# A two-layer trunk on one core: the input projection's first four output tiles accumulated side by side, k outermost

## The reference

```python
def conv_pool_mixer(xn, w_in, ...):                  # layer 0
    proj = xn @ w_in                                 # 512 x 1024 by 1024 x 2048
    h, gate_b, gate_c, pin = jnp.split(proj, 4, axis=-1)
    ya = gate_b * causal_dwconv3(gate_c * h, conv_w)
    pooled = windowed means of pin (2, 4, 8, 16), less pin
    yb = pooled @ pool_w, per group of 128 channels, scaled
    return concatenate([ya, yb]) @ w_out

for layer in (0, 1):
    x = x + mixer(rmsnorm(x, g))                     # layer 1: dilated attention
    x = x + conv_glu_ffn(rmsnorm(x, g2))             # 1024 -> 5632 -> 2816 -> 1024
```

## Time and profile before

| | us |
|---|---|
| median of 3 runs | 1137.81 |
| lowest, highest | 1137.66, 1139.56 |
| the profiled execution: its time | 1137.77 |
| the profiled execution: its span | 1136.0 |

### The profile page before, as it was taken

One profiled execution on the slowest core, in us unless ns is written; L12 is line 12 of the kernel. 1 busy time (PEld: TensorE's weight loads), 2 busy tenths in 40 slices (PEclk: granted clock), 3 DMA queues, 4 the chain that ended last, 5 costly groups with the idle time before them and its releaser, 6 DMA issues.

```text
span 1136.0 us, 16020 instructions
## 1 busy us (share of the span) xinstructions
PE 1126.4 (99%) x5222; PEld 935.3 (82%) x5222; DVE 586.1 (52%) x1046; ACT 488.4 (43%) x750; POOL 460.8 (41%) x220
## 2 busy tenths in 40 slices
PE   8999999999999999999999999999999999999998
PEld 5788888888888888888888888878888888888887
DVE  6885755454454512215777777777844545450000
ACT  5323444444443432224666666544544444441220
POOL 3543534544435355542222233134544454435442
PEclk9999999999999999999999999999999999999999
DMA  7232323223222233332322223222332222323332
GB/s 247 78 125 77 111 74 112 92 92 111 84 101 84 63 112 93 99 113 65 91 83 78 74 74 99 77 74 77 127 106 81 108 92 92 95 63 102 102 98 77
DMA packets 35901, 108.11 MB, mean 95 GB/s; under 512 B 4192, under 2 KB 4192, under 8 KB 35872
## 3 DMA queue, kind: packets, MB, share of 16 engines
q1 hardware_dynamic: 33536, 103.49, 27.8%
q10 hardware_dynamic: 2336, 4.24, 1.3%
HBM read 105.57 MB, written 2.15 MB: 95 GB/s over the span
## 4 chain that ended last, share of the span: by engine, by line
issue 45%; PE 33%; POOL 20%; DMA 1%; POOLq 0%; ACT 0%; SPq 0%; DVE 0%; DVEq 0%
POOL wl L412 20%; PE bank L1040 7%; PE bank L1039 7%; PE bank L1038 7%; PE spt L1038 4%; PE spt L1039 4%; PE spt L1040 4%; DMA x<-xt 1%; POOLq L411 0%; POOLq L417 0%; ACT xh L452 0%; PE obank L1040 0%; PE obank L1039 0%; PE obank L1038 0%; ACT wh L442 0%
## 5 line engine op out<-in xcount | busy, mean ns | idle before, releaser
L412 POOL TENSOR_TENSOR wl<-raw,wh 128x1024 fp32r<-128x1024 f32 (+2 forms) x214 | 457.3, 2143 | 649.8 <-ACT wh L442 649.8
L1038 PE MATMUL bank<-xh,wh 128*128 128x512 f32 x1024 | 404.0, 395 | 1.9 <-DVE wl L749 1.9
L1040 PE MATMUL bank<-xh,wl 128*128 128x512 f32 x1024 | 399.8, 390 | 0.0
L1039 PE MATMUL bank<-xl,wh 128*128 128x512 f32 x1024 | 399.3, 390 | 0.0
L442 ACT ACTIVATE wh<-raw 128x1024 fp32r<-128x1024 f32 (+1 forms) x215 | 202.3, 946 | 144.1 <-PE spt L1040 139.5
L1038 PEld LDWEIGHTS bank<-xh,wh 128*128 128x128 f32 x1024 | 192.7, 188 | 42.4 <-DVE wl L749 2.8
L1040 PEld LDWEIGHTS bank<-xh,wl 128*128 128x128 f32 x1024 | 192.5, 188 | 40.2
L1039 PEld LDWEIGHTS bank<-xl,wh 128*128 128x128 f32 x1024 | 192.8, 188 | 38.6
L861 DVE TENSOR_TENSOR work<-bank,rstd 128x512 f32<-128x512 f32 x88 | 60.5, 691 | 225.7 <-PE bank L1040 223.8
L1038 PE MATMUL spt<-bh,wh 128*128 128x512 f32 x440 | 171.5, 390 | 0.4 <-POOL wl L412 0.3
L1039 PE MATMUL spt<-bl,wh 128*128 128x512 f32 x440 | 171.2, 389 | 0.0
(11 more groups left out here) (139 smaller groups left out, 887.0 us busy)
## 6 DMA issues: line engine op xcount, KB each, us to landing
raw<-w_up SPq DMA_DIRECT2D x88, 512.0 KB, 3.2
raw<-w_down SPq DMA_DIRECT2D x32, 384.0 KB, 3.1
raw<-w_down SPq DMA_DIRECT2D x32, 320.0 KB, 2.8
raw<-w_qkv SPq DMA_DIRECT2D x16, 512.0 KB, 3.4
raw<-w_in SPq DMA_DIRECT2D x15, 512.0 KB, 3.3
raw<-w_out SPq DMA_DIRECT2D x8, 512.0 KB, 3.2
raw<-w_qkv SPq DMA_DIRECT2D x16, 256.0 KB, 2.7
work<-bias_rows ACTq DMA_DIRECT2D x16, 256.0 KB, 3.1
```

The costliest lines, as they stand in the source:

```text
L412: nc.gpsimd.tensor_tensor(wl[s][:, 0:n], raw[s][:, 0:n], plain(wh[s][:, 0:n]), ALU.subtract).then_inc(s_lo, 1)
L1038: mm(dst, wh[s][:, w], hi, start=first, stop=False)
L1039: mm(dst, wh[s][:, w], lo, start=False, stop=False)
L1040: return mm(dst, wl[s][:, w], hi, start=False, stop=last)
```

## The change

**Loads.** x comes tile by tile (8 transfers of 256 KB). The first four units come k-wise: slot 0 holds k = 0 and 1 of tiles 0 to 3, slot 1 k = 2 and 3, and so on. The first four chunks (one k, four tiles, 256 KB) are single transfers whose rows are 512 B; slots 2 and 3 are loaded as pairs (512 KB, rows of 1 KB). x tiles and chunks alternate. The semaphores for halves become one per slot.

**TensorE.** Six warm-up matmuls of 256 columns instead of three of 512. For k = 0 to 5: four matmuls wh by xh into banks 0 to 3, four wh by xl, four wl by xh, each four with its own wait. Then, tile by tile, k = 6 and 7 (`first_end`). `norm_stats` stands after tile 0's end, `norm_spread` after tile 2's, the two bias products after tile 3's.

**The other engines.** VectorE rounds the very first chunk (`tensor_copy`) and forms its rest; ScalarE rounds the other chunks, GpSimd forms the other rests. ScalarE squares x tiles between its roundings; VectorE adds them between the rests of x, with the running sum in a PSUM bank (`first_acc`), and the last add goes to `acc`. ScalarE rounds unit 4 before the pooling weights and the norm's copy instead of after them. On VectorE the bias vectors and the pooling weights' rest move behind group 0; some memsets move to the start. The DMA of the bias rows on ScalarE's queue moves from group 0 to group 1. Some work buffers change places.

```diff
-WARM = 3
+WARM = 6
...
+        def chunk(buf, kk):
+            return buf[:].rearrange("p (j k n) -> p j k n", j=4, k=2)[:, :, kk, :]
...
+            def first_rows(k0, k1):
+                return w_in[0:4, :, k0 * P:k1 * P].rearrange("j p n -> p j n")
...
-            x_load(0)
-            sp.dma_start(raw[0][:, 0:SLOT // 2], w_in[0, :, 0:SLOT // 2]).then_inc(s_raw_a, 16)
-            load(0, 0, raw[0][:, SLOT // 2:], w_in[0, :, SLOT // 2:], True)
-            x_load(1)
-            load(1, 1, raw[1][:], w_in[1], True)
-            x_load(2)
-            x_load(3)
-            load(2, 2, raw[2][:], w_in[2], True)
+            for u in range(2):
+                x_load(2 * u)
+                half_load(u, 0, s_raw_a[u])
+                x_load(2 * u + 1)
+                half_load(u, 1, s_raw[u])
+            x_load(4)
+            pair_load(2)
+            x_load(5)
+            x_load(6)
+            pair_load(3)
+            x_load(7)
             sp.dma_start(par[:, C_FFN:], params[:, C_FFN:]).then_inc(s_par_b, 16)
-            load(3, 3, raw[3][:], w_in[3], True)
...
+            pool.wait_ge(s_hi, 1)
+            rest_first(0, 1).then_inc(s_lo, 1)
+            pool.wait_ge(s_hi_a[1], 1)
+            rest_first(1, 0).then_inc(s_lo_a[1], 1)
+            pool.wait_ge(s_hi, 2)
+            rest_first(1, 1).then_inc(s_lo, 1)
...
             round_first(0)
             round_first(1)
             act.wait_ge(s_raw[0], 16)
+            round_chunk(0, 1).then_inc(s_hi, 1)
+            square_first(0)
             round_first(2)
+            act.wait_ge(s_raw_a[1], 16)
+            round_chunk(1, 0).then_inc(s_hi_a[1], 1)
+            square_first(1)
             round_first(3)
+            act.wait_ge(s_raw[1], 16)
+            round_chunk(1, 1).then_inc(s_hi, 1)
+            square_first(2)
+            round_first(4)
             round_unit(0, 2, True)
+            square_first(3)
+            round_first(5)
+            square_first(4)
+            round_first(6)
+            round_unit(0, 3, True)
+            round_first(7)
+            for k in range(5, KT):
                 square_first(k)
+            ahead(U_IN, 0, 1)
...
+            dve.wait_ge(s_raw_a[0], 16)
+            nc.vector.tensor_copy(chunk(wh[0], 0), chunk(raw[0], 0)).then_inc(s_hi_a[0], 1)
             rest_x(0, 0)
+            dve.wait_ge(s_hi_a[0], 1)
+            nc.vector.tensor_tensor(chunk(wl[0], 0), chunk(raw[0], 0), plain(chunk(wh[0], 0)),
+                                    ALU.subtract).then_inc(s_lo_a[0], 1)
+            rest_x(0, 1)
+            for k in range(2, KT):
                 rest_x(0, k)
+                add_first(k - 2, first_acc)
+            add_first(KT - 2, first_acc)
             dve.wait_ge(s_warm, 1)
+            add_first(KT - 1, acc[:])
             norm_rsqrt(0)
...
-                last = mm(obank[:], acc[:, 0:P], acc[:], start=True, stop=True)
+                last = mm(obank[:, 0:SEQ // 2], acc[:, 0:P], acc[:, 0:SEQ // 2], start=True, stop=True)
...
+            for k in range(KT - 2):
+                early = k < 4 and k % 2 == 0
+                pe.wait_ge(s_xh, k + 1)
+                if early:
+                    pe.wait_ge(s_hi_a[k // 2], 1)
+                else:
+                    pe.wait_ge(s_hi, k // 2 + 1)
+                for j in range(4):
+                    mm(bank[j][:], first_weight(wh, j, k), xh[:, k, :], start=k == 0, stop=False)
+                pe.wait_ge(s_xl, k + 1)
+                for j in range(4):
+                    mm(bank[j][:], first_weight(wh, j, k), xl[:, k, :], start=False, stop=False)
+                if early:
+                    pe.wait_ge(s_lo_a[k // 2], 1)
+                else:
+                    unit_ready(U_IN + k // 2)
+                for j in range(4):
+                    last = mm(bank[j][:], first_weight(wl, j, k), xh[:, k, :], start=False, stop=False)
+                if k % 2:
                     last.then_inc(s_unit, 1)
...
+            pe.wait_ge(s_xl, KT)
+            unit_ready(U_IN + 3)
+            first_end(0)
             pe.wait_ge(s_par_b, 16)
             norm_stats(0)
+            first_end(1)
+            first_end(2)
+            norm_spread(0)
+            first_end(3)
             pe.wait_ge(s_setup, 48)
```

More of the change, by code:

```diff
@@ L221, in trunk @@
         s_warm = sem("s_warm")
-        s_xin = [sem(f"s_xin{n}") for n in range(4)]
+        s_xin = [sem(f"s_xin{n}") for n in range(KT)]
         s_pool = sem("s_pool")
@@ L372, in _ @@
             sp.dma_start(poolraw, poolw).then_inc(s_pool, 16)
-            sp.wait_ge(s_lo_a, 2)
+            for u in range(2):
+                sp.wait_ge(s_lo_a[u], 1)
             with sp.Fori(1, GROUPS) as i:
@@ L419, in rests, with rest_first @@
                         rest(i * RING + (first + s), s, sizes[s])
[L421 to L425, removed]
+            def rest_first(u, kk):
+                return nc.gpsimd.tensor_tensor(chunk(wl[u], kk), chunk(raw[u], kk), plain(chunk(wh[u], kk)),
+                                               ALU.subtract)
+            pool.wait_ge(s_hi, 1)
[4 more added lines that the diff above has]
+            rest_first(1, 1).then_inc(s_lo, 1)
             for s in range(2, RING):
@@ L499, in _ @@
                     ahead(U_IN, g, 0)
-                ahead(U_IN, g, 1)
+                    ahead(U_IN, g, 1)
                 act.wait_ge(s_zc, g + 1)
@@ L776, in _, with bias_vectors @@
[L776 to L784, removed]
-                                    ALU.subtract).then_inc(s_pwl, 1)
+            def bias_vectors():
+                dve.wait_ge(s_setup, 48)
+                dve.wait_ge(s_bvmm, 2)
+                heads = 2 * PAIRS
+                link(nc.vector.tensor_tensor(bv_sb[0:heads, 0:SEQ], obank[0:heads, :],
+                                             cnt_sb[0:heads, 0:SEQ], ALU.add))
+                nc.vector.tensor_tensor(bv_sb[0:heads, SEQ:NVEC], rbank[0][0:heads, 0:NVEC - SEQ],
+                                        cnt_sb[0:heads, SEQ:NVEC], ALU.add).then_inc(s_bv, 1)
+                dve.wait_ge(s_bv, 1)
+                link(nc.vector.memset(pb[:, 0:PAD], 0.0))
@@ L1083, in _ @@
             for n in range(WARM):
-                last = mm(obank[:], acc[:, 0:P], acc[:], start=True, stop=True)
+                last = mm(obank[:, 0:SEQ // 2], acc[:, 0:P], acc[:, 0:SEQ // 2], start=True, stop=True)
             last.then_inc(s_warm, 1)
-            def in_part(j, k0, k1):
-                for k in range(k0, k1):
-                    last = product(bank[j][:], j, k, xh[:, k, :], xl[:, k, :], k == 0, k == KT - 1)
-                if k1 == KT:
-                    last.then_inc(s_unit, 1)
@@ new lines, in first_end @@
+            def first_end(j):
+                for k in range(KT - 2, KT):
+                    mm(bank[j][:], first_weight(wh, j, k), xh[:, k, :], start=False, stop=False)
+                    mm(bank[j][:], first_weight(wh, j, k), xl[:, k, :], start=False, stop=False)
+                    last = mm(bank[j][:], first_weight(wl, j, k), xh[:, k, :], start=False, stop=k == KT - 1)
+                last.then_inc(s_first if j < 3 else s_unit, 1)
+            pe.wait_ge(s_xl, KT)
+            unit_ready(U_IN + 3)
```

100 lines of the change are left out of this document (42 added, 58 removed).

## The result

| | before | after |
|---|---|---|
| median, us | 1139.56 (7 runs) | 1132.62 (7 runs) |
| lowest to highest | 1137.66 to 1142.45 | 1132.41 to 1132.86 |
| the profiled execution, time and span | 1137.77, 1136.0 | 1132.44, 1130.6 |
| T1, first matmul of tile 4 | 36.96 | 31.61 |

The changed kernel takes 0.9942 of the time, 95% interval 0.9928 to 0.9955. Of the profiled executions it is 5.33 us shorter, and T1 is 5.35 us earlier: all of it is won in the opening and kept. By medians it is 6.9 us, since the kernel before scatters by 5 us and the changed one by half a microsecond.

The account below looks back on a forecast made before the run. TensorE's passage through the first four output tiles sets the time. T1 = 6.8 + 21.8 + 0.98 + 2.3 + 0.35 = 32.3, 4.66 us earlier (start 1.4, clock 1.8, waiting 1.8, less 0.35): 1133.1 us, range 1132.1 to 1136.0.

Parts of the forecast that it names:

- the fixed rest: Behind the statistics up to T1: two bias products, spread of the norm, longer steps; 2.3 us, expected to stay.
- The start: First projection matmul at 6.8 us instead of 8.23, set by first chunk landing at 6.2; 1.4 us gained.
- The 2 us allowed for uncovered weight loads: Warm-up: uncovered weight loads in the extra matmuls could add under 2 us to its expected end at 6.28.
- The packets: Opening loads: estimated 29 ns per 512 B packet and 47 ns per 1 KB, against 20 and 40.
- Rival (d): Opening loads: small k-wise packets become the bound, from 86 ns each T1 is past 36.96; 1141.1 us, chance 0.06.
- the kept clock: First ten projection matmuls: a shorter standstill ahead keeps TensorE's clock full; 1.8 us gained.
- the waiting that goes: TensorE at the sum of squares: its wait for VectorE's last add disappears; 1.8 us gained.
- rival (a): Opening: the clock still falls after a late first chunk, so 1.8 us are lost; 1134.9 us, chance 0.12.
- The sum of squares: VectorE's last add, helped by its PSUM operand, ends near 24.3, 0.2 us ahead of TensorE's statistics at 24.5.
- Rival (b): Late opening: GpSimd's unit 4 rest delays VectorE's xl by 1 us, last add by 0.7; 1134.8 us, chance 0.20.
- Cost nothing, under that cover: Bias vectors and pooling weights' rest behind group 0 on VectorE: no cost, 16.2 us against TensorE's 21.8 per group.
- Rival (c): Group 1: unit 5's rest, hanging on VectorE's group 0 work, takes up the gain; 1137.8 us, chance 0.07.

Follow-up runs that it names:

- The kernel with the clock kept: The kernel before with four warm-up matmuls of 512 columns instead of three, nothing else; median 1139.23 us, ratio 0.9999 to the kernel before.

## Why the prediction was right, and where a step of it was not

**T1 and the sum.** Predicted 32.3 for T1 and 1133.1 us; measured 31.61 and 1132.62 (1132.44 in the profiled execution). That the gain in the opening is kept whole was right: 5.35 us at T1, 5.33 us in the time. The sum of TensorE's own work held: 6.51 + 21.8 (96 steps) + 0.4 (the first matmul's step, 0.63 us instead of 0.23, the clock being still at half) + 0.8 (statistics) + 2.1 (the fixed rest, 25.45 to 31.61 less 18 steps) = 31.6. The statistics were given 0.98 and the fixed rest 2.3. The allowance of 0.35 for small waits was not needed.

**The start.** Predicted 6.8, measured 6.51, by another bound. The chunk was in by 5.28, not 6.2: from 2.2 to 4.0 us the queue moved 225 GB/s instead of the 193 of the earlier trace rows, which accounts for a part of it; the rest is not explained. The warm-up's end set the start. Its last pass began at 6.44 where that of the kernel before began at 5.68, since the clock rose only at 6.9 and not at 5.3. This moment changes from execution to execution: in two of the variants above with the same warm-up (the sum in SBUF, the bias vectors first) the clock rose at 4.6 and at 6.2, and the first matmul stood at 6.00 and at 6.36. That 6.51 lies so near to 6.8 is partly luck. The 2 us allowed for uncovered weight loads did not come: at half clock a pass of 256 columns takes 0.427 us and one of 512 columns 0.853. The packets came close to the estimate. The DMA view of the changed kernel from 5 to 9 us:

```profile
DMA packets 1463, 1.14 MB, mean 285 GB/s; under 512 B 69, under 2 KB 1185, under 8 KB 1463
...
q1 hardware_dynamic: 1463, 1.14, 97.5%
```

These are 1116 packets of 512 B, 278 of 2 KB and 69 small ones in 62 us of engine time (97.5% of 16 x 4). The times of the single packets in the trace are 27 ns for 512 B (mean), against an estimate of 29, and 46 ns for 1 KB (mean from 10.5 to 11 us), against 47. By the Trainium skill (DMA: Bandwidth & Descriptors, Why small descriptors are slow) 512 B take 19 cycles instead of 16, an estimate of 24 ns on the 4 KB rate's 20; the trace has a little more. Rival (d) needed 86.

**The clock: the step that failed.** The prediction counted 1.8 us gained by the kept clock and 1.8 us by the waiting that goes, as two terms of a sum. In TensorE's own budget both are there, but they are not two causes. The kernel with the clock kept gained 0.2 us at T1; the kernel with the sum in PSUM gained 2.4 us by itself. And the 1.8 us were not all the clock's: with full clock the first ten matmuls still took 3.43 us and not 2.27, because they waited for a rest of x. Before, T1 hung on VectorE's adds: 26.1 for the last one, and behind the statistics 10.7 us of TensorE's work, 33 of the matmuls among them. Time that TensorE lost ahead of it was time that it would have waited. What the change does is therefore better told so: the statistics start 1.6 us earlier (26.24 to 24.64), 15 more matmuls stand ahead of them (78 instead of 63, 3.4 us), and the rest is 0.3 us shorter. The total was right because after the change TensorE is the bound from end to end, and its own work can be summed; the same sum on the kernel before only lists where its time went. The 1.8 us of rival (a) were sized right for the changed kernel, where half clock costs what it takes: the executions with four warm-ups differ by up to 1.8 us. But what happens there is a clock that rises late, not one that falls in the pause.

**The sum of squares.** Right in mechanism and close in size: the last add was to end near 24.3, margin 0.2; it ended at 23.97, margin 0.67. The rows' reading, that an add from PSUM is not held up, is borne out by the same adds in SBUF, which took up to 2.9 us beside GpSimd. The Trainium skill (SBUF — State Buffer, Who interferes with whom) has GpSimd and a VectorE instruction with two SBUF inputs exclude each other, and one with a single SBUF input go free; each of these meetings agrees.

**Rival (b)** did not happen, by 0.58 us, and costs 1.3 us (median) where it does. Its ground against it, that unit 4's load comes later, fits: ScalarE waited 0.83 us for that load, until 20.45.

**What moved behind.** "Cost nothing, under that cover" holds: put back, each costs its wait (1.3 and 2.8 us) plus, in many executions, half clock. Unit 5's rest ended at 36.18, expected near 35.5, due at 37.1. Rival (c) did not come.

**What was missed** is the scatter. The range and the chances stood on the profiled execution of before and three runs. By medians the gain is 6.9 us, not 4.7, because the changed kernel has no pause left that the clock can fall behind: its seven executions all have a mean clock of 1.000. The row of 1139.56 among three runs was the sign.

## What to carry to other kernels

A budget of the busiest engine's idle and slow time is a list of places, not of causes: before adding two entries, ask for each which chain ends the wait behind it, for time won ahead of a wait is given to the wait. A pause on TensorE can cost more than its length, since the clock may fall behind it: the two pauses of 2.8 us cost 1.7 and near 3 us more. Times that stand in steps are a sign to look for, and the mean granted clock of each execution tells whether half clock makes them. And where GpSimd and VectorE share a stage, the sum that VectorE keeps was safer in PSUM here, and the order of the last few instructions is better held by a wait than by a margin of half a microsecond.

## What the runs showed of the hardware that was not expected

In one execution of the kernel with the sum in PSUM (1137.55 us) the clock fell to half far from any opening, from 548.6 to 552.0 us, at the start of the attention, where the profile shows no wait but many small matmuls (of 2 and of 128 columns) just ahead of it. The profile of the kernel before has the same matmuls there and no fall. Busy by stretch:

```profile
548.00:550.00 2.00, 2.00 (x10) 1.81 (x10) 1.73 (x9) 0.00 (x0) 0.30 (x1) 0.64 0.70 238
550.00:552.00 2.00, 2.00 (x9) 1.81 (x8) 1.48 (x4) 0.00 (x0) 0.00 (x0) 0.50 0.61 238
```

And the column of the granted clock shows 1.00 ahead of its first change, where the steps tell another thing: the warm-up matmuls of the changed kernel follow each other at half rate (twelve passes, most 0.427 us apart, the last from 6.44), and the four projection matmuls at 6.00 in the kernel with four warm-ups take 2.04 us. At the start of a trace the clock is to be read from the steps.
